# Block-wise neighbourhood attention with gathered values, and softmax units taken in pairs, in a four-layer fp32 kernel

## What is computed

```python
col_idx = np.clip(np.arange(ncb) * NA_QW - NA_KW // 2, 0, GRID_W - NA_CB)[:, None] + np.arange(NA_CB)[None, :]
...
s_loc = jnp.einsum('bhrnqkc'...) * scale + bias
s_ctx = jnp.einsum('bhrnql'...) * scale
p = jax.nn.softmax(jnp.concatenate([s_loc, s_ctx], axis=-1), axis=-1)
o = p_loc @ v_blk + p_ctx @ vc
```

## Time and profile before

| | us |
|---|---|
| runs, median of 3 | 4304.98 (4283.55 to 4305.91) |
| the profiled execution | 4286.57 |
| its span in the trace | 4284.2 |
| PE busy | 3678.6 (86%) |
| DVE busy | 2041.0 (48%) |
| ACT busy | 1119.0 (26%) |

### The profile page before, as it was taken

One profiled execution on the slowest core, in us unless ns is written; L12 is line 12 of the kernel. 1 busy time (PEld: TensorE's weight loads), 2 busy tenths in 40 slices (PEclk: granted clock), 3 DMA queues, 4 the chain that ended last, 5 costly groups with the idle time before them and its releaser, 6 DMA issues. The chain is left out here.

```text
span 4284.2 us, 50945 instructions
## 1 busy us (share of the span) xinstructions
PE 3678.6 (86%) x20742; PEld 3051.4 (71%) x20742; DVE 2041.0 (48%) x3759; ACT 1119.0 (26%) x1867; POOL 2.7 (0%) x8
## 2 busy tenths in 40 slices
PE   6996998999997987989997984688998883778997
PEld 5986777788886976777875972466887772456886
DVE  3235665433334235664444448754334448664333
ACT  2121443211112131442221321323222321323222
POOL 0000000000000000000000000000000000000000
PEclk9995899999998985999998995779999895679999
DMA  5320000332241200015444320014443320002332
GB/s 188 124 91 5 22 1 30 99 114 85 93 126 62 80 20 25 1 34 169 133 143 125 97 62 0 1 30 137 138 150 125 101 75 0 1 25 74 94 98 74
DMA packets 313562, 326.88 MB, mean 76 GB/s; under 512 B 11211, under 2 KB 229875, under 8 KB 313203
## 3 DMA queue, kind: packets, MB, share of 16 engines
q1 hardware_dynamic: 313330, 323.64, 24.7%
HBM read 321.50 MB, written 2.10 MB: 76 GB/s over the span
## 5 line engine op out<-in xcount | busy, mean ns | idle before, releaser
L1271 DVE TENSOR_TENSOR weights_low<-weights,weights_high 128x1024 fp32r<-128x1024 f32 (+4 forms) x424 | 485.2, 1147 | 1290.7 <-ACT weights_high L933 1288.9
L933 ACT ACTIVATE weights_high<-weights 128x1024 fp32r<-128x1024 f32 (+4 forms) x424 | 422.3, 998 | 1429.6 <-PE bank L493 994.4
L850 PE MATMUL bank<-h_high,weights_high 128*128 128x512 f32 (+1 forms) x1760 | 658.8, 374 | 10.6 <-DVE h_low L1283 9.4
L850 PE MATMUL bank<-h_low,weights_high 128*128 128x512 f32 (+1 forms) x1760 | 649.9, 369 | 0.0
L850 PE MATMUL bank<-h_high,weights_low 128*128 128x512 f32 (+1 forms) x1760 | 648.9, 369 | 0.0
L493 PE MATMUL bank<-weights_high,h_high 128*128 128x426 f32 (+3 forms) x1424 | 519.7, 365 | 19.1 <-DVE h_low L1283 19.1
L493 PE MATMUL bank<-weights_high,h_low 128*128 128x426 f32 (+3 forms) x1424 | 512.7, 360 | 0.0
L493 PE MATMUL bank<-weights_low,h_high 128*128 128x426 f32 (+3 forms) x1424 | 512.5, 360 | 0.0
L850 PEld LDWEIGHTS bank<-h_high,weights_high 128*128 128x128 f32 x1760 | 333.0, 189 | 84.0 <-DVE h_low L1283 17.0
L850 PEld LDWEIGHTS bank<-h_high,weights_low 128*128 128x128 f32 x1760 | 333.0, 189 | 56.0
L850 PEld LDWEIGHTS bank<-h_low,weights_high 128*128 128x128 f32 x1760 | 333.4, 189 | 51.9
(11 more groups left out here) (243 smaller groups left out, 4158.3 us busy)
## 6 DMA issues: line engine op xcount, KB each, us to landing
projected<-in_w_mod SPq DMA_DIRECT2D x80, 1024.0 KB, 5.3
weights<-in_w_gate_up SPq DMA_DIRECT2D x88, 512.0 KB, 4.0
weights<-in_w_down SPq DMA_DIRECT2D x80, 512.0 KB, 3.9
weights<-in_w_in SPq DMA_DIRECT2D x80, 426.0 KB, 3.4
weights<-in_w_gate SPq DMA_DIRECT2D x44, 512.0 KB, 6.7
weights<-in_w_up SPq DMA_DIRECT2D x44, 512.0 KB, 7.7
weights<-in_w_mod SPq DMA_DIRECT2D x32, 512.0 KB, 3.9
weights<-in_w_out SPq DMA_DIRECT2D x32, 512.0 KB, 3.6
```

What stands on the lines that cost most here:

```text
L850: mm = pe.matmul(bank[:, 0:cnt], wt[:, k, :], x[:, k, a:a + cnt], start=(k == 0 and q == 0), stop=(k == KD - 1 and q == 2))
L933: act.activation(WH[s_ % 2][:, 0:k * n], slots[j % LAND][:, 0:k * n], ACT.Copy).then_inc(S["w_high"], 1)
L1271: dve.tensor_tensor(WL[s_ % 2][:, 0:k * n], slots[split_of[s_] % LAND][:, 0:k * n], WH[s_ % 2][:, 0:k * n].bitcast(F32), ALU.subtract).the ...
```

## The change

Neighbourhood attention takes its queries in four blocks of 16 columns x 8 rows, so a unit has 256 context keys and 256 grid keys (8 rows x 32 columns, a strided view of the turned keys). The values of such a block do not lie together in SBUF: the grid's values are stored to DRAM after the input projection and gathered back with 32 DMAs of 32 rows. The bias comes ready from DRAM in six units of 512 KB; no one-hot matmuls remain. The queries are scaled by 0.125 when they are copied. Two units of different row halves of PE make a pair: their scores matmuls alternate and write different banks, both units' blocks are turned, then the next pair's scores are issued, then both units' values (64 columns instead of 128). One DVE instruction adds the bias and takes the maximum. The output of 6 (or 8) heads of a tile is divided in one instruction. Sliding-window and masked attention go through the same function; the mLSTM keeps its own. The sink is handled beside the scores instead of as an extra column. The output projection's input is put back in the order of the rows when it is copied.

```diff
-W_IN_ORDER = [(0, 256), (768, 256), (1056, 384), (2208, 384), (256, 512), (1024, 32), (1440, 768), (2592, 256)]
+W_IN_ORDER = [(0, 256), (768, 256), (1056, 384)] + [(2208 + 64 * h, 64) for h in (0, 3, 1, 4, 2, 5)] + [(256, 512), (1024, 32), (1440, 768), (2592, 256)]
...
-        for j in range(8):
-            unit(w["onehot"][:, UNIT * j:UNIT * (j + 1)], 1, UNIT, split=False)
+        bias_units = [len(weight_units) + j for j in range(6)]
+        for j in range(6):
+            unit(w["bias"][j], 1, UNIT, split=False)
...
+        GATHERED = [pr(t, N_V, 384) for t in range(CTX_T, NT)] + [pr(t, G_K, 384) for t in range(CTX_T, NT)]
...
+        for n in range(4):
+            v = (0, 1, 1, 2)[n]
+            start = min(max(16 * n - 8, 0), 32)
+            for h in range(NA_H):
+                b, f = 64 * (h % 2), h // 2
+                near = KN[b:b + 64, f, 256:768].rearrange("p (r c) -> p r c", c=64)[:, :, start:start + 32]
+                zeros = slots[bias_units[2 * v + h // 3] % LAND]
+                both = bass.AP(tensor=zeros.tensor, offset=zeros.offset, ap=[list(zeros.ap[0]), [256 * (h % 3 + 1), 2], [1, 256]])
+                units.append(dict(q=QN[b:b + 64, f, 256 + 128 * n:384 + 128 * n], at=0, keys=[(0, KN[b:b + 64, f, 0:256]), (256, near)],
+                                  n=512, bias=both, table=2 * v + h // 3, sink=None, slot=h, size=6,
+                                  v=[pr(s, N_V + 64 * h, 64) for s in range(CTX_T)]
+                                  + [GATHERED[2 * n + i][:, 64 * h:64 * h + 64] for i in range(2)], y=pr(CTX_T + n, N_Q, 384)))
+        for t in OUT_T:
+            for i in range(SWA_H):
...
+                h, b, f = 3 * (i % 2) + i // 2, 64 * (i % 2), i // 2
+                u = dict(q=QS[b:b + 64, f, t * 128:(t + 1) * 128], at=256, keys=[(256, KS[b:b + 64, 0:256])], n=256,
+                         bias=MASKS[:, 0:256], table=None, sink=h, slot=h, size=6,
+                         v=[pr(s, S_V + 64 * (i % 2), 64) for s in range(CTX_T)], y=pr(t, S_Q, 384))
                 if t >= CTX_T:
                     lo, hi = max(t - 1, CTX_T), min(t + 2, NT)
-                    u["kb"] = KS[b:b + 64, kv, lo * 128:hi * 128]
-                    u["bias"] = CN[:, C_SW + (lo - t + 1) * 128:C_SW + (hi - t + 1) * 128]
-                    u["v"] += [(s, S_V + 64 * kv) for s in range(lo, hi)]
-                sw_units.append(u)
-        phases = [na_units, sw_units]
+                    u["keys"].append((512, KS[b:b + 64, lo * 128:hi * 128]))
+                    u["n"] += 128 * (hi - lo)
...
+                def scores(p):
+                    if p >= 1:
+                        pe.wait_ge(S["mix_max"], 2 * p)
+                    a, b = units[2 * p], units[2 * p + 1]
+                    for (at, ka), (_, kb) in zip(a["keys"], b["keys"]):
+                        cnt = ka.size() // ka.shape[0]
+                        pe.matmul(PSA[:, at:at + cnt], a["q"], ka, start=True, stop=True)
+                        mm = pe.matmul(PSA[:, 1024 + at:1024 + at + cnt], b["q"], kb, start=True, stop=True)
+                    mm.then_inc(S["mix_scores"], 1)
...
+                def turned(i):
+                    nb = units[i]["n"] // PT
+                    pe.wait_ge(S["mix_exp"], i + 1)
+                    if i >= 2:
+                        pe.wait_ge(S["mix_turned_dve" if i % 2 == 0 else "mix_turned_act"], i // 2)
+                        if n_fifth(units, i):
+                            pe.wait_ge(S["mix_fifth"], n_fifth(units, i))
+                    for j in range(nb):
+                        dst = PS[4 + i % 2][:, j * PT:(j + 1) * PT] if j < 4 else PS[6][:, (i % 2) * PT:(i % 2 + 1) * PT]
+                        mm = pe.transpose(dst, SB[i % 4][:, j * PT:(j + 1) * PT], ident)
...
+                def values(i):
+                    u = units[i]
+                    pe.wait_ge(S["mix_turned_dve" if i % 2 == 0 else "mix_turned_act"], i // 2 + 1)
+                    if u["n"] > 512:
+                        pe.wait_ge(S["mix_fifth"], n_fifth(units, i + 2 - i % 2))
+                    g = group_of(units, i)
+                    if g and first_of_group(units, i):
+                        pe.wait_ge(S["mix_out"], g)
+                    out = PS[7][:, 64 * u["slot"]:64 * u["slot"] + 64]
+                    for j, v in enumerate(u["v"]):
+                        mm = pe.matmul(out, PB[i % 2][:, j * PT:(j + 1) * PT], v, start=(j == 0), stop=(j == len(u["v"]) - 1))
+                    mm.then_inc(S["mix_values"], 1)
...
+                scores(0)
+                for p in range(len(units) // 2):
+                    turned(2 * p)
+                    turned(2 * p + 1)
+                    if p + 1 < len(units) // 2:
+                        scores(p + 1)
+                    values(2 * p)
+                    values(2 * p + 1)
+                pe.wait_ge(S["mix_out"], group_of(units, len(units) - 1) + 1)
...
-                pe.wait_ge(S["late"], n_late)
-                bank = B.fill(pe, "d")
-                pe.transpose(bank[0:31, 0:90], RPR, ident[0:90, 0:90]).then_inc(S["filled"], 1)
-                B.all_emptied(pe)
-                n = 0
-                for j in range(8):
-                    oh = next_unit()[0:32, 0, :].rearrange("p (c q) -> p c q", q=PT)
-                    for g in range(2):
-                        bank = B.fill(pe, turn[n % 2])
-                        n += 1
-                        for i in range(4):
-                            mm = pe.matmul(bank[:, 128 * i:128 * i + 128], oh[:, 4 * g + i, :], RPT, start=True, stop=True)
-                        mm.then_inc(S["filled"], 1)
-                    used()
...
+                for f in range(3):
+                    turn_columns(lambda t: pr(t, N_K + 128 * f, 128), ["d"])
+                turn_columns(lambda t: pr(t, S_K, 128), ["d"])
+                for j in range(6):
+                    release.append(("mix_max", n_of_table[j]))
+                pe.wait_ge(S["gathered"], 16 * 32)
+                softmax_attention()
...
+                    PB6.all_emptied(sp)
+                    sp.dma_start(w["v_na"].rearrange("(t p) n -> p t n", p=PT), PW[:, CTX_T:, N_V:N_V + 384]).then_inc(S["v_saved"], 16)
+                if not second and j == bias_units[0] + LAND:
+                    sp.wait_ge(S["v_saved"], 16)
+                    for i in range(8):
+                        if i == 4:
+                            sp.wait_ge(S["rope"], 1)
+                            sp.dma_start(MASKS, w["masks"]).then_inc(S["masks"], 16)
+                        start = min(max(16 * (i // 2) - 8, 0), 32)
+                        for r in range(4):
+                            row = 64 * (4 * (i % 2) + r) + start
+                            sp.dma_start(GATHERED[i][32 * r:32 * r + 32, :], w["v_na"][row:row + 32, :]).then_inc(S["gathered"], 16)
...
+                def exp(i):
+                    u, c = units[i], i % 16
+                    act.wait_ge(S["mix_max"], i + 1)
+                    act.activation(SB[i % 4][:, 0:u["n"]], SB[i % 4][:, 0:u["n"]], ACT.Exp, scale=-1.0, bias=NMX[:, c:c + 1],
+                                   accum_out=RSM[:, c:c + 1]).then_inc(S["mix_exp"], 1)
...
+                for p in range(len(units) // 2):
+                    u = units[2 * p + 1]
+                    nb = min(u["n"], 512)
+                    act.wait_ge(S["mix_turn"], 2 * p + 2)
+                    if p:
+                        act.wait_ge(S["mix_values"], 2 * p)
+                    act.activation(PB[1][:, 0:nb], PS[5][:, 0:nb], ACT.Copy).then_inc(S["mix_turned_act"], 1)
+                    if u["n"] > 512:
+                        for e in range(2):
+                            ins = act.activation(PB[e][:, 512:640], PS[6][:, 128 * e:128 * e + 128], ACT.Copy)
+                        ins.then_inc(S["mix_fifth"], 1)
+                    if 2 * p + 3 < len(units):
+                        exp(2 * p + 2)
...
+                        dve.wait_ge(S["landed%d" % (j % LAND)], 16 * (j // LAND + 1))
+                    dve.wait_ge(S["mix_scores"], i // 2 + 1)
+                    if i >= 4:
+                        dve.wait_ge(S["mix_turn"], i - 3)
+                    to, src = SB[i % 4][:, 0:n], PSA[:, a:a + n]
+                    if len(u["bias"].shape) == 3:
+                        to, src = to.rearrange("p (b c) -> p b c", b=2), src.rearrange("p (b c) -> p b c", b=2)
+                    first = 3.0e38 if u["sink"] is None else NSINK[:, u["sink"]:u["sink"] + 1]
+                    dve.tensor_tensor_reduce(to, src, u["bias"], -1.0, first, ALU.add, ALU.min, NMX[:, c:c + 1]).then_inc(S["mix_max"], 1)
...
+                    size, g = units[i]["size"], group_of(units, i)
+                    dve.wait_ge(S["mix_exp"], i + size)
+                    for q in range(size):
+                        k, u = (i + q) % 16, units[i + q]
+                        ins = dve.tensor_copy(RCP[:, u["slot"]:u["slot"] + 1], RSM[:, k:k + 1])
```

(17 more changed lines are left out.)

473 lines of the change are left out of this document (218 added, 255 removed).

## The result

The median of four runs is 4041.24 us (4037.83 to 4043.45) against 4302.29 (4283.55 to 4305.91) for the kernel before, a ratio of 0.9401 [0.9372, 0.9429]. The profiled execution took 4041.36 and its span is 4039.6: 245 us less than the profiled execution before, where the sum gave 216. The forecast of 4080 lies 39 us above the median, inside the range.

What follows compares the result with a forecast made beforehand. PE was taken to bound the attention stages, mostly on masked keys. Layer gains of 102, 86, 12 and 16 us sum to -216 on 4286.6, giving 4071; the forecast was put at 4080, range 4030 to 4155.

Steps and rivals of the forecast that it cites:

- The table goes, -30 and -29: Neighbourhood attention of layers 1 and 2: without building the bias table, attention starts 30 and 29 us sooner.
- The gather at nothing: Start of attention in layers 1 and 2: late gather DMAs hidden behind head_norm and column copies, costed at nothing.
- Rival 5: The 17 late gather DMAs land one after another, 7.1 us each; +107 us per layer, 4285, no change; chance 0.03.
- A pair of 512 at 4.1: Attention at full clock: the dependency chain makes a pair with 512 keys per unit take 4.1 us; two units took 7.26.
- the 0.62 among its signs: Sign that the forecast is right: the custom DVE instruction takes near 0.62 us for 512 elements.
- The row halves overlap: Scores in attention: alternating PE row halves overlap almost fully, 1.2 us taken, between bounds of 0.85 and 2.05.
- rival 1: PE's row halves take turns on the scores; each pair pays 1.67 ns per key more, 4138 us; chance 0.13.
- rivals 1 and 2: Row halves take turns, 4138 (chance 0.13); DVE's instruction at half rate from PSUM, 41 us more, 4112 (chance 0.07).
- Clock at 0.50 for 15 us at the start of L1 and L2: Assumption in the sum: PE runs at half clock for the first 15 us of attention in layers 1 and 2.
- Clock at 0.50 for 30 us in L3, and up to the whole of L4: Masked attention: half clock for 30 us gives 63 us in layer 3; layer 4, up to all at half clock, 70.
- Rivals 3 and 4: Clock at 0.50 for about half the attention, 4190 (chance 0.12), or all of it, 4303, slower (chance 0.03).

Runs made afterwards that it cites:

- after: The changed kernel itself, with the whole change applied to the kernel before: median 4041.24 us, ratio 0.9401.
- one control: The changed kernel run again with nothing altered, beside a follow-up run on the same chip: 4038.16 us, ratio 0.9372.

## Why the prediction was right, and where it was off

The time, the sign and the chain were right. The gain was 245 us where the sum had 216, and nearly all of the difference is in L3 and L4, where two terms were too small.

- **The table goes, -30 and -29.** Right: measured alone, 33 and 32. In after, L1's attention starts at 420.1 for the 418 forecast, 2 us late, because GLA itself ended 3 us later than in the trace before.
- **The gather at nothing.** Right, shown by the run without it. Its loads land in 2.6 us, not in the 7.1 of the earlier trace rows that bounded them, but an issue takes 0.46 and not 0.31, and the first waited for a rotation that ended 3 us later: about 416.6 for the 415.6 forecast, with 3.5 us of room in L1 in place of 2. Rival 5 is out.
- **A pair of 512 at 4.1.** Right: 4.16. Scores about 1.1 for 1.2, DVE 0.69 for 0.70, both exponentials as priced. The rest too: 2.79 for 2.75 (256), 3.40 for 3.4 (384), 4.80 for 4.9 (640); at clock 0.50, 3.91 for 4.1 (256), 2.52 for 2.45 (128), 7.3 for 7.6 (512). Value passes did keep their pace: 16 in 2.00 us. Of the two figures that the prediction gave for the custom instruction, the 0.70 of its chain was right and the 0.62 among its signs was not.
- **The row halves overlap.** Right, read from two kinds of packed matmul; rival 1 would have paid 0.85 per pair, and the run on one half did. But rivals 1 and 2 were priced by their instructions alone, at 67 and 41 us. The run on one half lost 209, and a DVE twice as long lost 134, since the second exponential waits for both units' instructions and the clock stayed low for longer. By these runs, 4250 and 4176 us, either rival would have ended above the range's 4155.
- **Clock at 0.50 for 15 us at the start of L1 and L2.** 30 and 13. In L1 the first six pairs have 256 keys, and PE's clock rose 6 us after the pairs of 512 began; L2, which starts with pairs of 512, had it after 13 (that the pairs of 256 delayed it was not tried by itself, and the same L2 had it after 7 us in one control and after 30 in the run with long rows first). L1 started 2 us late and took 149 us for 147, which makes its -98 for -102; L2 gave -91 for -86 with 111 us for 113 and a start that came 3 us sooner than forecast.
- **Clock at 0.50 for 30 us in L3, and up to the whole of L4.** This is the step that was mis-sized: "30 in layers 3 and 4, where 34 us passed before the clock rose in layer 3". The sum had laid the low clock on the pairs of 128 and 256 keys and on two of 384 (its 18.4 is about 2 x 5.9 + 2 x 3.4, which is 38 us at half clock and not 30), and more in L4. Measured, the clock rose 25 us after the start of both, within the first pair of 384. Then 4 x 2.52, 4 x 3.91, 3.40 for three pairs of 384 and 4.14 for the first, 4.07 for those of 512 and an end make 57, where the sum had 63 and 70 (and full clock would have saved 19 us of those 70, not the 16 it names). I took the old stage's 34 us as if the time passed regardless of what ran. The change also reorders the masked attention by rows, as the whole diff shows (n outside, h inside), and what an order does to the clock I did not price. Rows alone, longest first, took the old kernel's stage from 75 and 86 to 58 and 58, next to the 57 of after; in the new kernel longest first is worth 6 us more than its own shortest first. The old kernel with its shortest rows first and the new one with the old mixed order did not run, so how much of the gain of L3 and L4 is the order and how much the pairs stays open.
- **Rivals 3 and 4**, the low clock, did not come true. They were close by: with 0.85 us more per pair the clock was at 0.50 for most of L2 and all of L3 and L4.

How -245 divides can be told only roughly, since each part was measured without the others: the table 65, the grid keys 54 (30 and 24), the row order in L3 and L4 up to 46 (18 and 28 from first scores to last values, with the longest rows first); what is left, some 80 us, is for the pairs, the merged instruction, the second round of turned columns and, in their wake, the clock. That the parts add up so was not tested.

## What to carry to other kernels

Where PE's clock moves between its two levels, price a change twice: once by its instructions, once by how long the stage would stand at half clock, and look at the order of long and short units as well as at their number. When work is moved ahead on one engine, read the next engine's program for the wait that it will now stand behind; here that made 54 us of loss out of an expected gain. One place later, with the exception of the 640 pairs and together with long rows first, it made a gain of 32. Two independent heads on the two row halves of PE were worth their full overlap here. And when a stage is cut out of a table for comparison, let it end with its own last instruction.

## What the runs showed of the hardware that was not expected

- Two fp32 matmuls on rows 0 to 63 and 64 to 127, issued in turn into different banks, start in the same 0.01 us (486.91 and 486.91) and run side by side, the four 256-column products of a pair within about 1.1 us, against 2.0 on one row half.
- The order of the same instructions alone changed the granted clock over a stage from 0.75 and 0.62 to 0.92 and 0.92 (stretches of 75, 86, 62 and 62 us), the stage from 75 and 86 to 58 and 58 us, and the whole kernel by 1.5%.
- The run on one row half stood at 0.50 for 157 us of L2's attention, in a stretch of 197 us of which PE was busy in 194.62.
- The same kernel had its clock back in L3 after 25 us in two executions and after 41 in a third, and in L2 after 7, 13 and 14 us.
- The custom DVE instruction takes 688 ns for 512 elements with a constant as its start value and 748 with a pointer to one; for 256 it is 423 and 481.
